# Linear attention's query and key products on GpSimd, masked copies in each step's second chunk, and chunks from selection round 14 on

## What is computed

```python
def gla_mixer(q, k, v, glog):              # 4 heads of 48, chunks of 64 tokens
    b = jnp.cumsum(gf, axis=2)             # sums of log gates within a chunk
    b_last = b[:, :, -1:]
    qe = qf * jnp.exp(b) * (dk ** -0.5)
    ke = kf * jnp.exp(-b)
    kd = kf * jnp.exp(b_last - b)
    A = jnp.where(tril, jnp.einsum('bnihd,bnjhd->bnhij', qe, ke), 0.0)
    o_intra = jnp.einsum('bnhij,bnjhv->bnihv', A, vf)
    U = jnp.einsum('bnjhd,bnjhv->bnhdv', kd, vf)
    # scan over chunks: S = exp(b_last) * S + U; o_inter = qe @ S of the chunk before
    ...
def dsa_mixer(q, k, v, q_idx, k_idx, w_idx, rel_bias):
    score = ...                            # one row of scores for each query
    _, idx = lax.top_k(score, topk)        # topk = 256
    # softmax attention over the picked keys
    ...
```

## Time and profile before

| | us |
|---|---|
| median of three runs | 2905.91 (2904.7 to 2911.28) |
| the profiled execution | 2904.64 |
| its span | 2902.8 |

### The profile page before, as it was taken

One profiled execution on the slowest core, in us unless ns is written; L12 is line 12 of the kernel. 1 busy time (PEld: TensorE's weight loads), 2 busy tenths in 40 slices (PEclk: granted clock), 3 DMA queues, 4 the chain that ended last, 5 costly groups with the idle time before them and its releaser, 6 DMA issues.

```text
span 2902.8 us, 41142 instructions
## 1 busy us (share of the span) xinstructions
PE 2792.1 (96%) x16908; PEld 2166.9 (75%) x16908; DVE 1184.7 (41%) x2813; ACT 902.8 (31%) x1701; POOL 1022.5 (35%) x447
## 2 busy tenths in 40 slices
PE   7999998899999999998999999999999999999998
PEld 5766675567777777776887878888888888887887
DVE  6989997556433333335335011111112121114323
ACT  5322413552333343344123122222222222224112
POOL 2542481133322222223632433333333333333531
PEclk8999998999999999999999999999999999999999
DMA  4110121121211111112121111111111111113211
GB/s 114 39 30 22 30 69 51 48 91 38 67 51 38 38 50 52 52 44 95 58 79 53 56 39 37 50 39 44 37 51 45 37 44 44 44 42 141 66 51 65
DMA packets 221334, 155.56 MB, mean 54 GB/s; under 512 B 25254, under 2 KB 207948, under 8 KB 221020
## 3 DMA queue, kind: packets, MB, share of 16 engines
q1 hardware_dynamic: 210076, 122.55, 14.6%
q10 hardware_dynamic: 11072, 30.39, 3.0%
HBM read 133.45 MB, written 19.47 MB: 53 GB/s over the span
## 4 chain that ended last, share of the span: by engine, by line
PE 51%; DVE 2%; issue 1%; ACT 1%; DMA 0%; ACTq 0%; DVEq 0%
PE proj L904 14%; PE proj L906 14%; PE proj L905 14%; PE out L1423 2%; PE score L1371 1%; PE score L1401 1%; PE score L1380 1%; PE proj L944 1%; PE out L905 0%; PE out L906 0%; PE out L904 0%; PE out L1390 0%; DMA y_scratch<-arena 0%; DVE arena L2343 0%; DVE arena L2470 0%
## 5 line engine op out<-in xcount | busy, mean ns | idle before, releaser
L904 PE MATMUL proj<-act_hi,w_hi 128*128 128x512 f32 x2560 | 1033.7, 404 | 10.4 <-ACT hT L1846 4.4
L906 PE MATMUL proj<-act_hi,w_lo 128*128 128x512 f32 x2560 | 1005.8, 393 | 0.0
L905 PE MATMUL proj<-act_lo,w_hi 128*128 128x512 f32 x2560 | 1005.3, 393 | 0.0
L777 POOL TENSOR_TENSOR w_hi<-w_raw,ones 128x1024 fp32r<-128x1024 f32 x175 | 420.6, 2403 | 1598.6 <-PE proj L906 1596.4
L904 PEld LDWEIGHTS proj<-act_hi,w_hi 128*128 128x128 f32 x2560 | 486.3, 190 | 122.8 <-issue 17.2
L906 PEld LDWEIGHTS proj<-act_hi,w_lo 128*128 128x128 f32 x2560 | 485.3, 190 | 104.7
L905 PEld LDWEIGHTS proj<-act_lo,w_hi 128*128 128x128 f32 x2560 | 486.6, 190 | 95.8 <-issue 0.2
L779 POOL TENSOR_TENSOR w_lo<-w_raw,w_hi 128x1024 fp32r<-128x1024 f32 x175 | 432.2, 2470 | 13.7
L1846 ACT ACTIVATE arena<-proj 128x512 f32<-128x512 f32 x236 | 175.9, 754 | 669.5 <-PE proj L906 645.5
L2470 DVE SCALAR_TENSOR_TENSOR arena<-arena,score 128x256 f32<-128x256 f32 (+1 forms) x192 | 76.1, 427 | 717.7 <-PE score L1371 676.9
L1872 ACT ACTIVATE arena<-score 128x512 f32<-128x512 f32 (+3 forms) x264 | 115.7, 486 | 197.9 <-PE score L1232 197.4
(11 more groups left out here) (268 smaller groups left out, 2874.1 us busy)
## 6 DMA issues: line engine op xcount, KB each, us to landing
w_raw<-dil_w_in_dram SPq DMA_DIRECT2D x80, 512.0 KB, 3.7
w_raw<-fox_w_in_dram SPq DMA_DIRECT2D x32, 512.0 KB, 4.1
w_raw<-w_in_dram SPq DMA_DIRECT2D x23, 512.0 KB, 3.8
y_scratch<-arena ACTq DMA_DIRECT2D x21, 512.0 KB, 3.6
act_lo<-y_scratch SPq DMA_DIRECT2D x21, 512.0 KB, 6.2
arena<-decay_scratch ACTq DMA_DIRECT2D x16, 512.0 KB, 5.9
w_raw<-ple_w_gate_dram SPq DMA_DIRECT2D x16, 512.0 KB, 3.7
arena<-x_dram SPq DMA_DIRECT2D x12, 512.0 KB, 5.0
```

The source lines that it names most:

```text
L777: pool.tensor_tensor(hi, raw, one.unsqueeze(1).broadcast_to([P, KB, P]), ALU.mult).then_inc(w_hi_done, 1)
L904: pe.matmul(bank, hi, a_hi, start=first, stop=False)
L905: pe.matmul(bank, hi, a_lo, start=False, stop=False)
L906: return pe.matmul(bank, lo, a_hi, start=False, stop=last)
```

## The change

`decayed_queries` and `chunk_keys` lose their four products on VectorE to GpSimd, where they stand ahead of the split of weight 7 and ahead of that of weight 9; `to_chunk_end` moves one weight later. The small copies of the chunk ends stay on VectorE. The masked copies are made in the second chunk of a step instead of the first. The first chunk comes after round 14 of tile 4 instead of round 12, so the last comes at (6, 12) instead of (6, 10). `inverse_roots` moves two rounds later, both `pool_outputs` and the last gated output one round earlier. Nothing is computed otherwise than before.

```diff
-GLA_ROUNDS = {4: range(12, 32, 2), 5: range(0, 32, 2), 6: range(0, 12, 2)}
-TURNED_AT = {(6, 24): 0, (6, 25): 1, (6, 27): 2, (6, 29): 3, (6, 30): 4, (7, 1): 5}
+GLA_ROUNDS = {4: range(14, 32, 2), 5: range(0, 32, 2), 6: range(0, 14, 2)}
+TURNED_AT = {(6, 24): 0, (6, 25): 1, (6, 27): 2, (6, 29): 3, (6, 30): 4, (7, 0): 5}
...
+            def decayed_queries():
+
+                pool.wait_ge(GL["eb"], 1)
+                for half in range(2):
+                    pool.wait_ge(pass_free[half], 6)
+                for b in range(2):
+                    pool.tensor_tensor(gq[:, b], gq[:, b], gb_e[:, b], ALU.mult).then_inc(GL["q"], 1)
+
+            def chunk_keys():
+
+                pool.wait_ge(GL["kdexp"], 1)
+                for half in range(2):
+                    pool.wait_ge(pass_free[half], 8)
+                for b in range(2):
+                    pool.tensor_tensor(gb_x[:, b], gb_x[:, b], gk[:, b], ALU.mult).then_inc(GL["kd"], 1)
...
-                       7: (lambda: heads(4, 2), to_chunk_end), 9: (lambda: heads(5, 0), decayed_keys), 10: (lambda: heads(5, 2),),
+                       7: (lambda: heads(4, 2), decayed_queries), 8: (to_chunk_end,), 9: (chunk_keys, decayed_keys, lambda: heads(5, 0)), 10: (lambda: heads(5, 2),),
...
-            def decayed_queries():
+            def chunk_ends():
                 dve.wait_ge(g["eb"], 1)
-                for half in range(2):
-                    dve.wait_ge(pass_free[half], 6)
-                for b in range(2):
-                    dve.tensor_tensor(gq[:, b], gq[:, b], gb_e[:, b], ALU.mult).then_inc(g["q"], 1)
...
             def gla_chunk(n, c):
                 t, b = n // 2, n % 2
-                if c == 0:
+                if c == 1:
                     for u in range(2):
...
-                          (4, 8): chunk_keys, (6, 13): inverse_roots, (7, 13): lambda: pool_outputs(0), (7, 26): lambda: pool_outputs(1)}
+                          (6, 15): inverse_roots, (7, 12): lambda: pool_outputs(0), (7, 25): lambda: pool_outputs(1)}
```

More of the change, by code:

```diff
@@ L2257, in beside @@
                 nonlocal chunk
-                pieces = {(2, 14): lambda: indexer_weights(obanks[0], 4, NT, 3), (3, 7): log_gates, (3, 10): gate_sums, (3, 18): decayed_queries,
-                          (4, 8): chunk_keys, (6, 13): inverse_roots, (7, 13): lambda: pool_outputs(0), (7, 26): lambda: pool_outputs(1)}
+                pieces = {(2, 14): lambda: indexer_weights(obanks[0], 4, NT, 3), (3, 7): log_gates, (3, 10): gate_sums, (3, 18): chunk_ends,
+                          (6, 15): inverse_roots, (7, 12): lambda: pool_outputs(0), (7, 25): lambda: pool_outputs(1)}
                 if (i, r) in pieces:
```

## The result

The changed kernel takes **2917.11 us** in the median of seven runs (2913.75 to 2922.21), the kernel before 2907.93 us (2904.7 to 2911.28). The ratio is 1.0032, 95% interval 1.002 to 1.0043: 9.2 us slower. In a second comparison it was 1.0035 (1.0022 to 1.0047), 10.3 us. Forecast were 4.2 us more, 2910.1 us, on a median of three runs of before, 2905.91 us.

The account below looks back on a forecast made before the run. TensorE was taken to bound the kernel up to the last chunk, then VectorE up to the last mask; -4.7 + 3.9 + 1.7 + 2.9 + 0.4 = +4.2 us on 2905.91 gave 2910.1 us, range 2903 to 2917.

Parts of the forecast that it names:

- What bounds the kernel: Up to 467.2 us: TensorE to the last chunk at 327.3 us, then VectorE's rounds; everything behind shifts equally.
- Term 1: VectorE behind the last chunk: two rounds fewer are left, -4.7 us.
- Terms 2 and 3: TensorE ahead of pass 8: idle while exp(-b) delays ScalarE's evacuation, +3.9 us; then a lower clock, +1.7 us.
- the evacuation doesn't hold TensorE: Rival at pass 8: no pause and no clock loss there, -1.4 us in all, 2904.5 us; chance 0.07.
- Terms 4 and 5: Masked copies in the second chunk: TensorE waits, mainly in step 0, +2.9 us; VectorE's last chunk ends later, +0.4 us.
- The sum: All five terms at the last mask: +4.2 us, 471.4 instead of 467.2 us.
- The range: Whole kernel's time, for 8 in 10: 2903 to 2917 us.
- The clock pays more: Rival in the linear attention: two more slow-clock stretches of 1.8 us each, +7.8 us, 2913.7 us; chance 0.3.
- VectorE was the bound of the steps: Rival in the linear attention's steps: VectorE's 8.5 us head start counts, -8.1 us, 2897.8 us; chance 0.1.

Follow-up runs that it names:

- the rounds alone: Kernel before with chunks from round 14 and what follows shifted as in the change; products on VectorE, copies in the first chunk: 2905.57 us.
- the filled after: Kernel after with four one-column memsets and five satisfied waits added on VectorE in the places of the removed products: 2914.4 us, ratio 1.0026 against before.

## Why the prediction was wrong

**What bounds the kernel** was right as far as 467 us: TensorE up to the last chunk, then VectorE up to the last mask. The failed step is the last sentence of that part: "Everything behind it is shifted by what that end is shifted." It is not: up to there after was 4.3 us late, and its median is 9.2 us higher. A shift of 1.3 us with nothing else changed became 5.9 in the median, and in the trace 6.9 at 800 us and 4.2 at 1600. The kernel before lies well in time: in its two profiles the 12.2 us behind the wait at 720 us have 56 and 55 matmul records, and no such stretch follows at 760.

**Term 1** (-4.7) measured -4.4 to -4.8 at the last mask. Of it 0.9 was given back at once in the rounds alone, since `pool_outputs` one round earlier only moved TensorE's wait to the end of the selection (1.9 to 4.5 us) and a longer stretch at the lower clock behind it. I had counted that edit as a gain.

**Terms 2 and 3** (+3.9, +1.7): the gap was 3.62 us and with the clock 5.4 us at the first step, so the clock took 1.8 us where 1.7 were forecast (mean granted clock 0.73 in the 5.6 us behind the gap, where near 0.6 was named). That it fits is in part luck: the 0.58 over 5.6 us of the earlier trace rows is worth 2.4 us by the clock (0.42 of 5.6), not the 1.8 that the prediction read from the count of matmuls. GpSimd's products took 4.75 us (4.77 taken), the split 2.38 (2.4 taken), the copy 0.19 (0.2 taken). The chain of reasons stands, and reordering ScalarE removes it; with it falls the rival that the evacuation doesn't hold TensorE.

**Terms 4 and 5** (+2.9, +0.4): waits of 3.04 and 3.32 us in steps 0 and 15 where 3.0 and 3 were named. Singly the copies cost 3.7 us at the last chunk and 3.0 at the last mask, where the two terms together were 3.3.

**The sum** up to the last mask was +4.2 and measured 4.3 and 4.4. That it fits so closely owes something to chance: the pause keeps only 2.9 of its 5.4 us when alone, and the two together cost 2.7 more than singly.

**The range** ended at 2917.0, and 2917.1 came. Of the 7.0 us between the forecast 2910.1 and this, 2.0 lie in the base: the forecast started from before's median of three runs, 2905.91, which was 2907.93 over seven. Against that base the miss is 5.0 us. "The clock pays more" (2913.7) had the sign and the engine, but put the two further stretches into the linear attention; they came behind 700 us. "VectorE was the bound of the steps" fell: with the products gone and nothing else, TensorE is at the first step to 0.1 us when before is.

**The account of the 9.2 to 10.3 us:** 4.3 up to the last mask. What a later arrival costs: 6.2 and 3.1 us between 600 and 800 us in the two profiles of after; in those of the kernels delayed by 1.3 and 3.9 us it is 6.3 and 3.1, and in their medians 4.6 and 2.3 over their delay. That nearly closes the sum: the two profiles of after are 10.3 and 7.2 us late at 1600 us. Shown is that a shift alone can make this second part. The costly kind of meeting with GpSimd at 1330 us is in neither profile of after. As it was missed by 0.06 and 0.03 us, other executions may well have it, and the filled after was 1.9 to 2.7 us lower, but within the noise; what it adds to after's median isn't shown. Why the stretch behind the same wait is 3 us long in one position and 12 in another stays open.

## What to carry to other kernels

In a kernel whose engines wait for one another in turn, a local gain or loss is not simply added at the end: compare both traces instruction by instruction behind the edit, and time a version with a pure delay of some microseconds, to learn what a shift alone does to this kernel. Work taken off an engine that waits anyway is worth nothing until later work is moved into the wait, and moving it must not hold up a third engine: here it was exp(-b), and one line of ScalarE's order gave back most of it. Where TensorE had to wait in two places for the same engine, one longer wait cost less than two middling ones, by 1.8 and 3.0 us at 600 us in two pairs of traces; that it lasts to the end is only a sign in the medians. And two engines that hold each other up may do so in the faster kernel too: ask which instruction is held, not only whether one is.

## What the runs showed of the hardware

- Behind the same wait of 4.4 us TensorE ran at 1.2 GHz for some 3 us in both profiles of before (mean granted clock 0.87 over 12.2 us), and for 12 us in the first of after and in the kernel delayed by 1.3 us (0.50). Before's two profiles keep within 0.3 us of each other, read every 100 us from 100 to 2600 us, so this is not mere scatter. The Trainium skill (TensorE: Matmul & The Clock Gate, its part on the clock gate) says that the moment of the change varies from run to run; the two profiles of after (36 and 42 records) agree with it, those of before do not show it.
- Four instructions and five waits fewer in VectorE's program made an instruction 1200 us later start 0.37 us later; fillers in their places undid it.
- A VectorE copy of 128 columns took 2.22 us against GpSimd's subtraction of 1024 columns, and 0.23 us otherwise; VectorE's own subtraction of 128 columns took 2.25 and 0.29 us. Starting 0.21 us ahead of GpSimd instead of 0.25 us behind it moved the hold from the one to the other, and TensorE's next wait from 1.05 to 3.17 us.
